# The first ten k tiles one at a time, fewer products of a constant tile, and two token loads on ScalarE's queue, in a hybrid transformer layer

## What is computed

```python
h = rms_norm(x, attn_norm_w)
proj = h @ w_in                       # 2048 x 5184
hq, hf, hi, hg, c_q, c_kv, k_r = split(proj)
o_a = hgrn2_mixer(hq, hf, hi, hg, ...)     # gated linear recurrence
o_b = mla_mixer(c_q, c_kv, k_r, ...)       # latent attention
x = x + concat([o_a, o_b]) @ w_out
h = rms_norm(x, ffn_norm_w)
gate, up = split(h @ w_gate_up)            # 2048 x 11264
x = x + (silu(gate) * up) @ w_down         # 5632 x 2048
```

## Time and profile before

| | us |
|---|---|
| median of 3 runs | 1107.96 |
| lowest, highest | 1107.83, 1108.14 |
| the profiled execution, its own time | 1108.18 |
| span of its trace | 1106.4 |
| TensorE busy in the span | 1099.8 |
| granted clock of the core in the profiled execution | 1.0 |

### The profile page before, as it was taken

The page is one execution under the profiler, slowest core; times in us unless marked ns, Lnnn a source line. Parts: engine busy times, 40 slices in busy tenths (PEclk is TensorE's granted clock), DMA queues, the critical chain, the costliest instruction groups (busy, mean ns, idle before and its releaser), DMA issues.

```text
span 1106.4 us, 15300 instructions
## 1 busy us (share of the span) xinstructions
PE 1099.8 (99%) x5154; PEld 926.2 (84%) x5154; DVE 903.4 (82%) x1250; ACT 645.0 (58%) x907; POOL 66.0 (6%) x164
## 2 busy tenths in 40 slices
PE   9999999999999999999999999999999999999998
PEld 9988888888888878888888888888888888888887
DVE  6688797587876587688888988988988889999887
ACT  6676766668654456365465455554554555654553
POOL 1500000000000010000100100001011010000000
PEclk9999999999999999999999999999999999999999
DMA  9866455454655486767777777777777777666655
GB/s 301 292 185 203 132 169 165 151 161 152 231 171 186 156 235 195 236 218 209 246 233 222 237 232 217 236 234 227 225 235 228 247 255 236 218 214 204 199 201 171
DMA packets 108083, 234.21 MB, mean 212 GB/s; under 512 B 8448, under 2 KB 17408, under 8 KB 107776
## 3 DMA queue, kind: packets, MB, share of 16 engines
q1 hardware_dynamic: 101360, 211.34, 59.1%
q0 software_dynamic: 6528, 22.03, 6.9%
q10 hardware_dynamic: 144, 0.20, 0.1%
HBM read 221.99 MB, written 11.53 MB: 211 GB/s over the span
## 4 chain that ended last, share of the span: by engine, by line
PE 97%; DVE 1%; ACT 1%; DMA 0%; issue 0%; SPq 0%; DVEq 0%; ACTq 0%
PE side L2036 24%; PE main L1802 21%; PE side L2038 12%; PE main L1805 11%; PE side L2006 4%; PE side L2008 4%; PE side L2007 4%; PE main L2006 3%; PE main L2008 3%; PE main L2007 3%; PE main L1822 1%; PE side L1928 1%; PE side L1844 0%; DMA raw<-in_w_in 0%; PE side L1879 0%; PE side L1880 0%
## 5 line engine op out<-in xcount | busy, mean ns | idle before, releaser
L1051 ACT CAST w_hi<-raw 128x1024 fp32r<-128x1024 f32 x245 | 239.7, 984 | 158.8 <-PE side L2036 85.4
L1640 DVE TENSOR_TENSOR w_lo<-raw,w_hi 128x1024 fp32r<-128x1024 f32 x245 | 274.2, 1131 | 13.9 <-ACT w_hi L1051 13.9
L1162 DVE TENSOR_TENSOR w_lo<-raw,w_hi 128x1024 fp32r<-128x1024 f32 (+3 forms) x156 | 178.7, 1155 | 94.4 <-ACT w_hi L829 93.1
L829 ACT CAST w_hi<-raw 128x1024 fp32r<-128x1024 f32 (+3 forms) x155 | 153.1, 996 | 127.1 <-PE main L1802 116.1
L1802 PE MATMUL main<-w_hi,hT_hi 128*128 128x512 f32 (+2 forms) x416 | 160.9, 388 | 0.0
L1805 PE MATMUL main<-w_hi,hT_lo 128*128 128x512 f32 (+2 forms) x416 | 157.6, 380 | 0.0
L2036 PE MATMUL side<-w_hi,hT_hi 128*128 128x512 f32 x400 | 155.6, 389 | 0.0
L2038 PE MATMUL side<-w_hi,hT_lo 128*128 128x512 f32 x400 | 155.6, 389 | 0.0
L1802 PE MATMUL main<-w_lo,hT_hi 128*128 128x512 f32 (+2 forms) x416 | 107.1, 379 | 0.0
L2036 PE MATMUL side<-w_lo,hT_hi 128*128 128x512 f32 x400 | 106.9, 389 | 0.0
L1805 PEld LDWEIGHTS main<-w_hi,hT_lo 128*128 128x128 f32 x416 | 78.2, 188 | 12.9
(11 more groups left out here) (308 smaller groups left out, 1890.1 us busy)
## 6 DMA issues: line engine op xcount, KB each, us to landing
raw<-in_w_gate_up SPq DMA_DIRECT2D x176, 512.0 KB, 4.7
raw<-in_w_down SPq DMA_DIRECT2D x88, 512.0 KB, 4.3
raw<-in_w_in SPq DMA_DIRECT2D x64, 512.0 KB, 4.3
raw<-in_w_out SPq DMA_DIRECT2D x32, 512.0 KB, 3.6
raw<-in_w_in SPq DMA_DIRECT2D x15, 384.0 KB, 5.5
squares<-hiddenT POOLq DMA_DIRECT2D x11, 512.0 KB, 4.5
hiddenT<-squares POOLq DMA_DIRECT2D x44, 128.0 KB, 5.4
raw<-in_w_ukv SPq DMA_DIRECT2D x8, 512.0 KB, 4.2
```

The lines of the kernel that those rows point to most:

```text
L829: copy(w_hi[:, slot, 0:n], raw[:, slot, 0:n]).then_inc(s_hi, 1)
L1051: copy(w_hi[:, n % RING, 0:cols], src).then_inc(s_hi, 1)
L1162: tt(w_lo[:, slot, 0:n], raw[:, slot, 0:n], w_hi[:, slot, 0:n].bitcast(F32), ALU.subtract)\
L1640: tt(w_lo[:, n % RING, 0:cols], src, w_hi[:, n % RING, 0:cols].bitcast(F32), ALU.subtract)\
```

## The change

The first block's pieces become ten of one k tile and three of two, thirteen granules instead of nine. FILLERS goes from 14 to 8. The loads of tokens follow the weights piece by piece: those of pieces 1 and 2 (k tiles 1 and 2, the second and third) are issued by ScalarE's queue behind granule 0, those of piece p from 3 on by SP's queue behind granule p. The table load of ScalarE comes behind its three DMAs. Every position behind the first block moves by four granules with `G0` and `END`; `X_AFTER`, `SMALL_AFTER` and the places of `sq1` and `r1` are moved by four by hand. `X_SPLIT` is written as a formula: pieces 0 and 1 at the first two positions, piece p from 2 on at position p - 3.

```diff
-PIECES = [(0, 1), (1, 1)] + [(k, 2) for k in range(2, KT, 2)]
+SINGLES = 10
+PIECES = [(k, 1) for k in range(SINGLES)] + [(k, 2) for k in range(SINGLES, KT, 2)]
...
-FILLERS = 14
-
-XT_AFTER = {1: (1,), 2: (2,), 3: (3, 4), 4: (5,), 5: (6,), 6: (7,), 7: (8,)}
-X_AFTER = {11: 0, 13: 1, 15: 2, 17: 3}
-SMALL_AFTER = 20
-
-X_SPLIT = (FIRST, FIRST + 1, -1, 0, 1, 2, 3, 4, 5)
+FILLERS = 8
+
+X_AFTER = {15: 0, 17: 1, 19: 2, 21: 3}
+BY_SCALAR = 2
+SMALL_AFTER = 24
+
+X_SPLIT = (FIRST, FIRST + 1) + tuple(p - LEAD for p in range(2, len(PIECES)))
...
-    s = [(at, ("sq1", c)) for c, at in enumerate((12, 14, 16, 18))]
-    s += [(19, ("r1a",)), (20, ("r1b",))]
+    s = [(at, ("sq1", c)) for c, at in enumerate((16, 18, 20, 22))]
+    s += [(23, ("r1a",)), (24, ("r1b",))]
...
-        def load_tokens(p):
+        def load_tokens(engine, p):
...
-            nc.sync.dma_start(dst, columns[:, c0:c1]).then_inc(s_xt[p], 16)
+            engine.dma_start(dst, columns[:, c0:c1]).then_inc(s_xt[p], 16)
...
-            load_tokens(0)
+            load_tokens(sp, 0)
...
-                for p in XT_AFTER.get(g, ()):
-                    load_tokens(p)
+                if BY_SCALAR < g < len(PIECES):
+                    load_tokens(sp, g)
...
             load_granule(act, 0)
+            for p in range(1, BY_SCALAR + 1):
+                load_tokens(act, p)
             table("natural_log_exp_and_others")
```

## The result

| | before | after |
|---|---|---|
| median, us | 1107.96 (1107.44 to 1108.39, 15 runs) | 1110.14 (1109.04 to 1111.69, 15 runs) |
| ratio of the medians | | 1.0019, 95% interval 1.0013 to 1.0026 |
| the profiled execution, its own time | 1108.18 | 1110.70 |
| span of its trace | 1106.4 | 1109.0 |
| start of tile 0 / of latent tile 1 | 6.38 / 24.34 | 4.56 / 25.06 |

A forecast was written before the change was run, and what follows sets the result against it. TensorE was taken as the bound, with at most 3.0 us to win in the opening. Tile 10 at 17.3 plus 6.24, 0.32 and 0.3 us ends the first block at 24.16 (-0.2 us): forecast 1107.8 us, range 1106.7 to 1109.9.

The forecast's parts named there:

- the ring's price: First block: waiting for ring slots eats most of the earlier start, leaving the block's end only 0.2 us sooner.
- What bounds the kernel, and the early start: Opening: TensorE bounds; tile 0 starts at 4.7 instead of 6.38, 1.7 us gained there, worth nothing unless later tiles follow.
- Tokens on ScalarE's queue: Opening: ScalarE issues three DMAs before its table load instead of one; cost nothing.
- from there on the programs are the same: Behind the first block: TensorE's start of latent tile 1 carries through to the end.
- Single tiles for ScalarE and VectorE: First block: ScalarE needs 1.0 us per tile against TensorE's 1.04; smaller conversions alone cost nothing.
- Tile 2: Opening: costs nothing if it lands before 6 us, 1.0 us if at 7.2; taken as +0.3 us.
- the early order does nothing: Rival, opening: tiles 2 and 3 land no sooner by ScalarE's queue; block ends at 24.86, time 1108.5; chance 0.05.
- The ring of four: First block: granule 6, landing after 3.1 us, holds back granule 10 (3.8 us); TensorE waits 1.4 us, tile 10 at 17.3.
- The end of the block: Last six tiles of the first block: 6.24 us plus 0.32 us lost by two-tile granules, behind tile 10's start.
- The sum: First block ends at 24.16 instead of 24.34, -0.2 us; bounds 23.36 (-1.0) and 25.96 (+1.6).
- The low clock: Rival, gaps between tiles 0 to 3: TensorE stays at 1.2 GHz until 14 us, +2.4 us, 1110.2; chance 0.05.
- From the trace to the median: Whole run: the profiled execution, 1108.18 us, lies 0.2 over the median 1107.96; its own time less 0.2 is 1108.0.

The follow-up runs named there:

- e1: The changed kernel once more, unchanged; median 1110.36 us, ratio 1.0019 to the kernel before.
- e2: The changed kernel with 14 products of the constant tile (FILLERS) instead of 8; median 1109.59 us, ratio 1.0019 to the kernel before.
- e6: The changed kernel with six more products of the constant tile, of 32 x 32 elements, behind its 8; median 1110.47 us, ratio 1.0023 to the kernel before.
- e8: The changed kernel with the tokens of k tiles 1 and 2 asked for by SP's queue again; median 1110.82 us, ratio 1.0024 to the kernel before.
- f3: The changed kernel with five products of the constant tile ahead of granule 10, in the place of TensorE's wait; median 1110.29 us, ratio 1.0017 to the kernel before.
- e3_before_fill8: The kernel before with 8 products of the constant tile (FILLERS) instead of 14; median 1108.47 us, ratio 1.0005 to the kernel before.
- e7_before_fill4: The kernel before with 4 products of the constant tile (FILLERS) instead of 14; median 1108.92 us, ratio 1.0005 to the kernel before.
- g4_half14_fill14: The changed kernel with singles in half slots of the ring, fourteen singles and 14 fillers; median 1107.67 us, ratio 0.9997 to the kernel before.
- g3_half14_again: f2_half_slots14 once more, unchanged (fourteen singles in half slots, 8 fillers); median 1106.71 us, ratio 0.9991 to the kernel before.
- f2_half_slots14: The changed kernel with singles in half slots of the ring and fourteen singles instead of ten; median 1107.01 us, ratio 0.9990 to the kernel before.
- f1_half_slots: The changed kernel with its ten singles in half slots of the ring; median 1108.06 us, ratio 0.9999 to the kernel before.
- g1: The kernel before with three products of the constant tile ahead of the first block's last granule; median 1108.68 us, ratio 1.0007 to the kernel before.
- g2: The kernel before with seven products of the constant tile ahead of the first block's last granule; median 1109.48 us, ratio 1.0015 to the kernel before.

## Why the prediction was wrong

The step that failed is the ring's price. The forecast put the landings of granules 6 and 10 at 3.1 and 3.8 us and so had the opening end 0.2 us sooner than before. In the six profiles with this ring and ten singles (the changed kernel, e1, e2, e6, e8, f3) they took 3.4 to 3.6 and 4.4 to 5.0 us, and latent tile 1 started between 25.06 and 26.90 instead of at 24.16. With half slots in the ring, and nothing else changed, the loss of 2 us was gone (1108.06 against 1108.30 for the kernel before). A second step failed with it: the one from a start in a single trace to the median of the runs.

- **What bounds the kernel, and the early start.** Right. Tile 0 was put at 4.7 and started at 4.56. That it is worth nothing unless the later tiles follow is what e3_before_fill8 and e7_before_fill4 showed, where nothing came of it, and g4_half14_fill14 against g3_half14_again, where it was worth a us.
- **Tokens on ScalarE's queue.** The cost of nothing holds for the opening (e8_no_scalar). Not foreseen: 0.3 us of ScalarE at 106 us and of TensorE at 135 us, in the kernels with both these DMAs and thirteen granules only. The step "from there on the programs are the same" had overlooked it.
- **Single tiles for ScalarE and VectorE.** Right: f2_half_slots14 ran fourteen of them at 0.8 to 1.0 us a tile, and TensorE waited for none.
- **Tile 2.** Put at +0.3 us for the chance that it lands late; it was in time, at 5.81. The rival that the early order does nothing did not have its condition: tiles 2 and 3 landed 0.5 and 0.7 us sooner than in e8_no_scalar. But the early order bought little, since latent tile 1 starts at 25.12 there, 0.06 us later than in the changed kernel.
- **The ring of four.** The mechanism, the granules (6 and 10), the tile and the order of its links were right; the sizes of two terms were not. Granule 6 landed after 3.57 us instead of 3.1, granule 10 after 4.41 instead of 3.8, so tile 10 started at 18.31 instead of 17.3. The reason given for 3.8, "the queue is not full", held when granules 5 to 8 were asked for (0.72 and 0.86 of the DMA engines from 6 to 10 us) and only in part for granule 10 (0.84 from 12 to 14 us, 0.99 from 14 to 16). It can't be the whole of it, for the row of 3.8 comes from a load that found them as busy (1.02 and 0.83 from 16 to 20 us before); what adds the 0.6 us stays open. It took 4.4 to 5.0 us in the other profiles with this ring, and 3.3 in f1_half_slots. 4.9 us stood among the rows, as the upper bound. The tokens of granule 10 had no term at all; in three profiles of six (e1, e2, f3) they were what TensorE waited for last.
- **The end of the block.** Put at 6.24 + 0.32 us behind the start of tile 10; it took 25.06 - 18.31 = 6.75, 0.2 more.
- **The sum.** 24.16 forecast, 25.06 measured: +1.0 for the landings, +0.2 for the last tiles, -0.3 for tile 2. It lies within the bounds of 23.36 and 25.96. This is 0.9 of the 2.3 us by which the time was missed. The measured sum is that of one profile, and an early one: the six profiles with this ring and ten singles have latent tile 1 at 25.6 in the mean.
- **The low clock.** A rival at 0.05, with its place in the opening's first gaps. The place was another: behind the wait ahead of tile 10, which the forecast had in its own sum, 1.4 us long. It is there in about one execution in five (11 of 59), and these take 1 to 3 us more. In e1_again, with the clock at its lower level for about 3 us, latent tile 1 came 1.8 us later than in the first profile.
- **From the trace to the median.** The forecast took the profile of before as typical but for 0.2 us. Neither its late tile 2 was typical, as the runs of the fillers and of displacement show, nor that it lost nothing near 900 us: the difference of latent tile 1 between two single profiles understated the difference of medians by some 0.8 us in most kernels. Averages fit better. The six profiles with this ring and ten singles start latent tile 1 at 25.61 us, the five of the old pieces (before, e3, e7, and g1 and g2 less what was put in) at 24.08: 1.5 us apart. With 0.3 us at 135 us, and 0.3 us between the means of what the two groups lose near 900 us (0.5 and 0.2), that makes 2.1 of the 2.2 us; the falls of the clock are in these means. They come from few profiles of unlike kernels, so this is a sum of the right size and not a proof; profiles of ten executions of each kernel would settle it, and were not made.
- **The range.** It took in the bounds of the landings and the runs' spread of 0.3 us, but nothing for the scatter of a single profile. Two profiles of the changed kernel have latent tile 1 at 25.06 and 26.90, and its runs spread over 2.65 us where those of before spread over 0.95. With 1.3 us, half of that spread, in place of the 0.3 us the range would have ended at 1110.9.

By the figures of the Trainium skill ("DMA: Bandwidth & Descriptors", the anatomy of one DMA), which are fitted for GpSimd's path, the two landings would take 2.4 and 2.9 us (an estimate). The trace has 3.57 and 4.41 for them, on SP's queue and with others under way, and the measurement decides.

## What to carry to other kernels

When pieces are made smaller in a ring with a fixed number of slots, count the bytes that can be under way, not the slots: halving the piece halves the prefetch, while a landing does not halve (here 3.6 us for 192 KB and 4.4 for 384 KB). Give small pieces half slots, and put the step from small to large pieces where the engine has cover. An earlier start pays only when no transfer behind it is late, and a change of this size needs the scatter of one profile in its range.

## What the runs showed of the hardware

- A wait of 1.98 us between stretches of dense products was followed by a granted clock of 0.50 for some 3 us, beginning a us after the work resumed (e1_again); the same kernel with 1.34 us showed 1.00 throughout its opening. Of 59 runs of kernels whose profile has a wait of 1.0 to 2.0 us at that place 11 had a mean clock of 0.998, of 110 runs of kernels without it none.
- One and the same 384 KB weight transfer of the opening, granule 10, took 3.3 us (f1_half_slots) to 5.0 us (e2_fill14), and 192 KB ones took 2.3 us (e1_again) to 5.2 us (f1_half_slots).
- With eight small loads under way the DMA engines moved 352 to 379 GB/s in this opening, with four 185 to 239 GB/s (f1_half_slots and the changed kernel, 6 to 10 us).
- ScalarE had 0.3 us more of idle time (1.96 instead of 1.67) ahead of one conversion near 106 us, in six profiles that have thirteen granules and two DMAs of ScalarE in common, and two conversions earlier (98.3 to 100.5 us) in the three with fifteen granules.
- The same 512 KB load of the down projection, near 890 us, landed after 5.0 to 9.2 us in 17 profiles, and where it took 7.4 us or more TensorE lost 0.25 to 1.65 us between 880 and 905 us. Code loads and the moves of `hiddenT` fall into the same microseconds; which of them delays it stays open.
